# Transposes issued one by one between the weight products, and the weight split one half load further ahead

## The chip, the cores and the metric

The kernel runs on one core of a Trainium2 chip. The metric is the device time of one execution in microseconds (us). TensorE (PE in the profile) multiplies and transposes into the accumulation banks; VectorE (DVE) and ScalarE (ACT) work on rows and banks; GpSimd (POOL) makes masks and scales a few tiles; SyncE (SP) issues the weight transfers. Each engine runs its own list of instructions in order, and they meet at semaphores.

## The reference

256 tokens of width 2048 pass through four layers in float32. The first block is a mixer and a feed-forward; the second is a gated delta net and a band attention:

```python
h = rms_norm(x, g);  proj = h @ w_in                      # 2048 x 9216
merged = g_a * (gmlp(uv) @ w_branch[:1024]) + g_b * (attn(q, k, v) @ w_branch[1024:])
x = x + merged @ w_out
up = conv3(rms_norm(x, g) @ w_up)                         # 2048 x 11008
x = rms_norm(x + (silu(gate) * val) @ w_down)
h = x + gated_deltanet(rms_norm(x)) @ w_out_a             # w_in 2048 x 8224, 16 heads of 128
h = h + chunk_band_attention(rms_norm(h)) @ w_out_b       # w_in 2048 x 8192
```

Nearly all arithmetic is in the products with the weights; attention, the delta rule, the convolutions and the norms are small beside them.

## The kernel before

**The stream of weights.** All weights are cut into tiles of 512 output columns, and each tile into half loads of up to two blocks of 128 rows (`stream_plan`). SyncE brings each half load into one of 4 `raw` slots. ACT rounds it to `w_hi` (line 416), DVE forms the rest `w_lo` (line 426), and TensorE makes three products for each block and each of two token halves: `x_hi*w_lo`, `x_hi*w_hi`, `x_lo*w_hi` (lines 447 to 449), so 12 products of 512 columns in a half load of two blocks. There are 4 slots of `w_hi` and `w_lo` (`SPLIT`): ACT may split half load m only when TensorE is done with m-4. TensorE accumulates tile t in one pair of `gemm` banks while ACT and DVE read the other.

**Side work.** Between half loads each engine does the rest of the kernel. It is written as generators ("sides") that stop at `yield`; one stretch up to a `yield` is called a stage here. `run(half, 8, side)` does a half load and then one stage of each side, eight times. On TensorE a stage is typically eight transposes of 128x128 (`turn_rows`, lines 1638 to 1645; `up_side`, `attend`, `conv_side`, `band` have their own loops), one semaphore increment behind the last of them, and a wait in front. They write the four `aux` banks; ACT and DVE copy these out in the stages after.

**How far apart the engines are.** ACT and DVE do `LOOK` = 2 half loads before their first stage. So their stage s stands behind half load s+2 of the same run of the loop, while TensorE's stage s stands behind its half load s. ACT's split of half load s+2 in turn needs TensorE to be done with s-2.

**The places that the prediction names.** `up_side` (lines 1798 to 1808): eight transposes of `up_rows` in the first stage of a tile. `delta` (lines 1871 to 1881): four stages in a row with eight transposes each, of `tmp`, `q_rows`, `k_rows`, `tmp`; each waits for the copies of the last one (DVE line 1378, ACT line 836) and for the scaled rows that DVE makes right behind its copy (line 1315). Still `delta`: the rows `o_rows` (DVE line 1450) are turned at line 1976 at the end of a group. There are four groups of heads, three of them in a loop. At the start, `hT_lo` (DVE line 1062) of each quarter of the input has to be there before the half loads that read it (lines 1676 to 1682). `load_bias` (line 613) lets ACT issue eight transfers at one place early on. `attend` and `band` turn the attention weights.

Of the kernel before, what the change touches and what calls it, by code (L numbers as in the profile page):

```python
# [24 lines left out]
TB = T // P  # L25
# [23 lines left out]
LOOK = 2  # L49
# [73 lines left out]
def program(nc, ins, out, parts=4):  # L123
    last_tile = {1: T_UP1, 2: T_A, 3: T_B, 4: N_TILES}[parts]
    last_half = TILE_END[last_tile - 1]
    with ExitStack() as ctx:
# [1505 lines left out]
        def _(pe):  # L1632
            pl = Place()
            half = lambda: pe_half(pe, pl)
# [12 lines left out]
            def x_turned(j, s, i):  # L1647

                b = 2 * s + i
                if b >= 4 or j:  # L1650
                    pe.wait_ge(S("hT_lo_done"), 8 * j + b - 3 if b >= 4 else 8 * j)
                turn_rows(x, (b % 4,), "hT_turned", 2 * b)

            def turn_x(j, s, t):

                yield
                pe.wait_ge(S("read_out0"), t + 1)
                pe.wait_ge(S("read_out1"), t + 1)
                x_turned(j, s, 0)
                x_turned(j, s, 1)  # L1660
                yield
                yield
                yield
# [8 lines left out]
            for s in range(2):  # L1672
                pe.wait_ge(S(f"x_landed{s}"), 16)
                for i in range(2):
                    x_turned(0, s, i)
            for load in range(4):
                if load < 2:
                    pe.wait_ge(S(f"x_landed{load + 2}"), 16)
                    for i in range(2):
                        x_turned(0, load + 2, i)  # L1680
                pe.wait_ge(S("hT_lo_done"), 2 * load + 2)
                run(half, 2)

            def mixing():
# [15 lines left out]
                for b in range(4):  # L1700
                    if b >= 2:
                        pe.wait_ge(S("ya_lo"), b - 1)
                    turn_rows(ug, (2 + b % 2,), "ya_turned", 2 * b)
                    yield

            def attend(g):
                for pr in range(4):
# [19 lines left out]
                    for a in range(2):  # L1727
# [5 lines left out]
                        m.then_inc(S("na_p_turned"), 1)  # L1733
# [3 lines left out]
                    for a in range(2):  # L1737
                        h = 2 * pr + a
                        for tb in range(TB):
                            for kb in range(TB):  # L1740
                                m = MM(AX[2 + a][:, tb * NAD:(tb + 1) * NAD], pT[:, a, kb, tb * P:(tb + 1) * P],  # L1741
                                       va[:, kb, h * NAD:(h + 1) * NAD], start=kb == 0, stop=kb == TB - 1)
                    m.then_inc(S("na_pv"), 1)
                    yield
                pe.wait_ge(S("na_out"), 4 * g + 4)
                turn_rows(yb, (2, 3), "yb_turned")
# [4 lines left out]
            def qkv_side(g, part):  # L1751
# [8 lines left out]
                turn_rows(qkv_tok, (0, 1), "qk_turned")  # L1760
# [21 lines left out]
            def turn_merged(n):  # L1782
                yield
                pe.wait_ge(S("merged"), n + 1)
                for b in (2 * n, 2 * n + 1):
                    if b >= 4:
                        pe.wait_ge(S("merged_lo"), b - 3)
                    turn_rows(ga, (b % 4,), "merged_turned", 2 * b)
# [9 lines left out]
            def up_side(t, n, width=2):  # L1798
# [3 lines left out]
                for b in range(2):  # L1802
# [4 lines left out]
                    m.then_inc(S("up_turned"), 1)  # L1807
# [34 lines left out]
            def conv_side(gi, part):  # L1842
# [8 lines left out]
                for i in range(2):  # L1851
                    turn_rows(tok, (i,), "c_turned", 2 * i)
# [5 lines left out]
                for tb in range(TB):  # L1858
                    for h in range(HG):
                        m = turn(AX[tb][:, h * P:(h + 1) * P], xc[:, h, tb * P:(tb + 1) * P], ident[:, :])  # L1860
                m.then_inc(S("c_back"), 1)
# [9 lines left out]
            def delta(gi):  # L1871
# [3 lines left out]
                for j, src in enumerate((tmp, qs, ks, tmp)):  # L1875
# [4 lines left out]
                    turn_rows(src, (2, 3), "d_turned")  # L1880
# [95 lines left out]
                turn_rows(o_rows, (2, 3), "d_y_turned")  # L1976
# [68 lines left out]
            def rows_side(gi, part):  # L2045
# [10 lines left out]
                turn_rows(tok, (0, 1), "b_turned")  # L2056
# [3 lines left out]
            def band(gi):  # L2060
                for _ in range(8):
                    yield
                for pr in range(2):
# [18 lines left out]
                    for a in range(2):  # L2082
# [4 lines left out]
                        m.then_inc(S("b_p_turned"), 1)  # L2087
# [13 lines left out]
                turn_rows(by, (2, 3), "b_y_turned")  # L2101
# [48 lines left out]
```

## Time and profile before

| | |
|---|---|
| median of 3 executions | 2628.32 us (2624.26 to 2629.22) |
| the profiled execution: first to last instruction (span) | 2623.4 us |
| what lies around the span, to the median | 4.9 us |
| TensorE busy | 2558.3 us, 98% |
| products with weights | 9480 of TensorE's 13782 instructions |
| instructions that multiply with `ident` (transposes) | 958 |
| DVE, ACT busy | 1493.5 us (57%), 1211.2 us (46%) |
| granted TensorE clock, mean | 0.993 |

The profiled execution has no timed value of its own beside its span, so the span is set against the median of the three timed ones. The profile's ends of matmuls are modelled: a product of 512 columns is shown with 0.39 us, though the next starts about 0.23 us after it. What an instruction costs TensorE is therefore read from one start to the next, never from its duration.

### The profile page before, as it was taken

What the parts mean: (1) busy time and instruction counts of PE and PEld (TensorE: products, weight loads), DVE (VectorE), ACT (ScalarE), POOL (GpSimd) and SP (SyncE); (2) the same over time, 40 slices, a digit from 0 to 9 for tenths busy, and PEclk for the clock granted to TensorE, in tenths of its full rate; (3) what the DMA queues carried; (4) which work ended last, traced back from release to release, by engine and by line L of the source; (5) the groups of instructions that cost most, each with busy time, mean ns of one, the idle gap of its engine ahead of it and who ended that gap; (6) DMA issues with size and microseconds to landing.
All of it is one profiled execution on the core that took longest, in us unless ns stands there. A gap on an engine that the chain in (4) does not pass through costs nothing.

```text
span 2623.4 us, 38136 instructions
## 1 busy us (share of the span) xinstructions
PE 2558.3 (98%) x13782; PEld 2096.0 (80%) x13782; DVE 1493.5 (57%) x1953; ACT 1211.2 (46%) x1830; POOL 106.2 (4%) x112
## 2 busy tenths in 40 slices
PE   7899999999999999999999999999999999999999
PEld 6688888888888888888887787877877678888887
DVE  5556555555666644666655655556473455555654
ACT  4435444444555533555444635335352335555543
POOL 0101100000200000000000110001101000000000
PEclk9899999999999999999999999999999999999999
DMA  7666555555656565555555433334332366556554
GB/s 243 192 192 161 165 180 186 181 191 192 215 177 188 178 198 194 180 182 181 180 188 161 145 98 113 108 101 123 104 114 73 96 190 189 156 177 190 158 179 161
DMA packets 286901, 431.40 MB, mean 164 GB/s; under 512 B 32560, under 2 KB 126000, under 8 KB 286640
## 3 DMA queue, kind: packets, MB, share of 16 engines
q1 hardware_dynamic: 264064, 414.25, 51.2%
q10 hardware_dynamic: 22704, 15.28, 2.2%
q8 instruction: 95, 1.56, 0.2%
q14 instruction: 38, 0.31, 0.0%
HBM read 427.37 MB, written 7.08 MB: 166 GB/s over the span
## 4 chain that ended last, share of the span: by engine, by line
PE 92%; DVE 3%; ACTq 1%; issue 1%; ACT 1%; DMA 1%; DVEq 0%; SPq 0%
PE gemm L447 27%; PE gemm L448 26%; PE gemm L449 26%; PE aux L1644 2%; PE aux L1924 1%; PE aux L1914 1%; PE aux L1923 1%; DVE w_lo L426 1%; PE aux L1967 1%; PE aux L1970 1%; PE aux L1806 1%; PE aux L1966 1%; DMA bbias<-band_bias_copies 1%; PE aux L1741 1%; ACTq L620 1%
## 5 line engine op out<-in xcount | busy, mean ns | idle before, releaser
L426 DVE TENSOR_TENSOR w_lo<-raw,w_hi 128x1024 fp32r<-128x1024 f32 (+1 forms) x800 | 967.4, 1221 | 607.4 <-ACT w_hi L416 597.9
L416 ACT ACTIVATE w_hi<-raw 128x1024 fp32r<-128x1024 f32 (+1 forms) x800 | 820.7, 1041 | 579.7 <-PE gemm L449 500.2
L447 PE MATMUL gemm<-w_lo,hT_hi 128*128 128x512 f32 (+1 forms) x2304 | 916.8, 398 | 19.3 <-DVE w_lo L426 18.6
L448 PE MATMUL gemm<-w_hi,hT_hi 128*128 128x512 f32 (+1 forms) x2304 | 897.3, 389 | 0.0
L449 PE MATMUL gemm<-w_hi,hT_lo 128*128 128x512 f32 (+1 forms) x2304 | 896.9, 389 | 0.0
L447 PEld LDWEIGHTS gemm<-w_lo,hT_hi 128*128 128x128 f32 x2304 | 434.2, 188 | 118.2 <-DVE w_lo L426 16.1
L449 PEld LDWEIGHTS gemm<-w_hi,hT_lo 128*128 128x128 f32 x2304 | 434.0, 188 | 91.7
L448 PEld LDWEIGHTS gemm<-w_hi,hT_hi 128*128 128x128 f32 x2304 | 434.7, 189 | 83.7
L447 PE MATMUL gemm<-w_lo,yT_hi 128*128 128x512 f32 x472 | 187.0, 396 | 0.8 <-DVE w_lo L426 0.8
L449 PE MATMUL gemm<-w_hi,yT_lo 128*128 128x512 f32 x472 | 186.4, 395 | 0.0
L448 PE MATMUL gemm<-w_hi,yT_hi 128*128 128x512 f32 x472 | 186.4, 395 | 0.0
L447 PE MATMUL gemm<-w_lo,zT_hi 128*128 128x512 f32 x256 | 105.1, 411 | 2.8 <-DVE zT_lo L1458 2.8
L447 PEld LDWEIGHTS gemm<-w_lo,yT_hi 128*128 128x128 f32 x472 | 88.6, 188 | 22.7 <-DVE w_lo L426 1.2
L449 PEld LDWEIGHTS gemm<-w_hi,yT_lo 128*128 128x128 f32 x472 | 88.6, 188 | 21.5
L448 PEld LDWEIGHTS gemm<-w_hi,yT_hi 128*128 128x128 f32 x472 | 88.6, 188 | 21.1
L448 PE MATMUL gemm<-w_hi,zT_hi 128*128 128x512 f32 x256 | 102.5, 400 | 0.0
L449 PE MATMUL gemm<-w_hi,zT_lo 128*128 128x512 f32 x256 | 102.3, 399 | 0.0
L1250 DVE TENSOR_TENSOR x_rows<-x_rows,gemm 128x512 f32<-128x512 f32 x40 | 25.7, 684 | 75.2 <-PE gemm L449 75.2
L1345 DVE SCALAR_TENSOR_TENSOR conv<-aux,conv_taps,conv 128x253 f32<-128x253 f32 (+1 forms) x144 | 62.5, 476 | 8.1 <-issue 6.1
L849 ACT ACTIVATE inverse<-aux 128x512 f32<-128x512 f32 x16 | 9.6, 599 | 117.7 <-PE aux L1924 117.7
L447 PEld LDWEIGHTS gemm<-w_lo,zT_hi 128*128 128x128 f32 x256 | 49.0, 191 | 15.2 <-DVE zT_lo L1458 3.0
L757 ACT ACTIVATE up_rows<-gemm,rstd 128x512 f32<-128x512 f32 (+1 forms) x22 | 15.0, 681 | 94.3 <-PE gemm L449 94.3
(298 smaller groups left out, 2187.1 us busy)
## 6 DMA issues: line engine op xcount, KB each, us to landing
raw<-in_w_up SPq DMA_DIRECT2D x336, 256.0 KB, 3.3
raw<-in_w_in SPq DMA_DIRECT2D x144, 512.0 KB, 4.3
raw<-in_a_w_in SPq DMA_DIRECT2D x128, 512.0 KB, 3.7
raw<-in_b_w_in SPq DMA_DIRECT2D x128, 512.0 KB, 4.1
raw<-in_w_down SPq DMA_DIRECT2D x76, 512.0 KB, 4.5
raw<-in_w_branch SPq DMA_DIRECT2D x32, 512.0 KB, 4.4
raw<-in_w_out SPq DMA_DIRECT2D x32, 512.0 KB, 4.3
raw<-in_a_w_out SPq DMA_DIRECT2D x32, 512.0 KB, 3.7
```

What stands on the lines that cost most here:

```text
L416: nc.scalar.activation(hi, src, ACT.Copy).then_inc(S("hi_done"), 1)
L426: nc.vector.tensor_tensor(lo, src, hi.bitcast(F32), ALU.subtract).then_inc(S("lo_done"), 1)
L447: nc.tensor.matmul(dst, xh, wl[:, k, :], start=h["start"] and k == 0, stop=False)
L448: nc.tensor.matmul(dst, xh, wh[:, k, :], start=False, stop=False)
L449: mm = nc.tensor.matmul(dst, xl, wh[:, k, :], start=False, stop=h["stop"] and k == h["n"] - 1)
L620: act.dma_start(bias[a * GRID:(a + 1) * GRID, u % BR, h, :, :], src).then_inc(S(f"bias_landed{u % BR}"), 16)
L1345: i = V.scalar_tensor_tensor(out=xc[:, 2 * b + e, back:], in0=src[:, 0:T - back], scalar=ctap[:, tap, bass.ds(gi * HG + (part * H + 2 * b ...
L1644: m = turn(AX[b][:, e * T + tb * P:e * T + (tb + 1) * P], src[:, tb, c:c + P], ident[:, :])
L1741: m = MM(AX[2 + a][:, tb * NAD:(tb + 1) * NAD], pT[:, a, kb, tb * P:(tb + 1) * P], va[:, kb, h * NAD:(h + 1) * NAD], start=kb == 0, stop=k ...
L1806: m = turn(AX[b][:, e * T + tb * P:e * T + (tb + 1) * P], ut[:, tb, c:c + P], ident[:, :])
L1914: m = MM(AX[2][rows_, c * C:(c + 1) * C], ATl[rows_, c, :], Tm[rows_, c, :], start=True, stop=True)
L1923: MM(AX[2][rows_, c * C:(c + 1) * C], Um[rows_, c, :], W1[rows_, c, :], start=True, stop=True)
```

## The change

Three things are changed.

`pe_half` takes the sides with it. After every single product it takes one step of each side (`slip`); what is left after the last product of the half load is done behind it. The generators now yield `True` after each transposition (and after each product of `attend`'s second part) and a bare `yield` still ends a stage. So a transposition stands behind the first product, the next behind the second, and so on.

`run` gives no side to its first half load, a stage to each following one, and does the last stage behind the last. So stage s is now spread over half load s+1; what is not a transposition (the small products of `delta`, the scores) still stands together, behind the first product of that half load.

`LOOK` is 3: ACT and DVE have half load s+3 behind them when they come to stage s.

```diff
-LOOK = 2
+LOOK = 3
...
-        def pe_half(pe, pl):
+        def pe_half(pe, pl, sides=()):
...
+            between = list(sides)
+
+            def slip():
+
+                between[:] = [s for s in between if next(s, None)]
+
...
                     nc.tensor.matmul(dst, xh, wl[:, k, :], start=h["start"] and k == 0, stop=False)
+                    slip()
                     nc.tensor.matmul(dst, xh, wh[:, k, :], start=False, stop=False)
+                    slip()
                     mm = nc.tensor.matmul(dst, xl, wh[:, k, :], start=False, stop=h["stop"] and k == h["n"] - 1)
-            mm.then_inc(S("half_done"), 1)
+                    if k == h["n"] - 1 and tb == TB - 1:
+                        mm.then_inc(S("half_done"), 1)
+                    slip()
+            while between:
+                slip()
...
+            def run(half, halves, *sides):
+
+                for i in range(halves):
+                    half(sides if i else ())
+                for s in sides:
+                    while next(s, None):
+                        pass
...
             def turn_rows(src, banks, event, at=0):
 
+                left = 4 * len(banks)
                 for i, b in enumerate(banks):
                     for e in range(2):
                         for tb in range(TB):
                             c = (at + 2 * i + e) * P
                             m = turn(AX[b][:, e * T + tb * P:e * T + (tb + 1) * P], src[:, tb, c:c + P], ident[:, :])
+                            left -= 1
+                            if left:
+                                yield True
                 m.then_inc(S(event), 1)
```

The callers of `turn_rows` become `yield from turn_rows(...)`, and the loops with transposes of their own get a `yield True` behind each.

The first place is TensorE in the loop over the tiles of `w_up`, around the first stage of a tile. Before:

```order
L449 MATMUL gemm<-w_hi,hT_lo 128x512
L1799 REGISTER_ALU
L1806 MATMUL aux<-ident,up_rows 128x128 [waits read_out1,read_out0]
L1806 MATMUL aux<-ident,up_rows 128x128 x7
L439 REGISTER_ALU
L447 MATMUL gemm<-w_lo,hT_hi 128x512 [waits lo_done]
L448 MATMUL gemm<-w_hi,hT_hi 128x512
```

And now, where the waits of the side stand behind the first product of the half load:

```order
L439 REGISTER_ALU
L453 MATMUL gemm<-w_lo,hT_hi 128x512 [waits lo_done]
L1829 REGISTER_ALU
L1836 MATMUL aux<-ident,up_rows 128x128 [waits read_out1,read_out0]
L455 MATMUL gemm<-w_hi,hT_hi 128x512
L1836 MATMUL aux<-ident,up_rows 128x128
L457 MATMUL gemm<-w_hi,hT_lo 128x512
L1836 MATMUL aux<-ident,up_rows 128x128
L453 MATMUL gemm<-w_lo,hT_hi 128x512
L1836 MATMUL aux<-ident,up_rows 128x128
```

The eight transposes stood together between two half loads; now each has a product on either side, and the eighth stands behind the eighth of twelve products.

The second place is TensorE in `delta`, where the transposes of `q_rows` follow those of `tmp`. Before, twelve products stood between the last of `tmp` and the first of `q_rows`, of which the last three are shown:

```order
L447 MATMUL gemm<-w_lo,hT_hi 128x512
L448 MATMUL gemm<-w_hi,hT_hi 128x512
L449 MATMUL gemm<-w_hi,hT_lo 128x512
L1876 REGISTER_ALU
L1644 MATMUL aux<-ident,q_rows 128x128 [waits d_out1,d_out0,d_rows]
L1644 MATMUL aux<-ident,q_rows 128x128 x7
```

Now these stand between them:

```order
L1665 MATMUL aux<-ident,tmp 128x128
L457 MATMUL gemm<-w_hi,hT_lo 128x512
L453 MATMUL gemm<-w_lo,hT_hi 128x512
L455 MATMUL gemm<-w_hi,hT_hi 128x512
L457 MATMUL gemm<-w_hi,hT_lo 128x512
L439 REGISTER_ALU
L453 MATMUL gemm<-w_lo,hT_hi 128x512 [waits lo_done]
L1911 REGISTER_ALU
L1665 MATMUL aux<-ident,q_rows 128x128 [waits d_out1,d_out0,d_rows]
```

Five products are left between the last transposition of one stage and the first of the next.

The third place is DVE at the start, where the splits of the first half loads and the quarters of `hT_lo` take turns. Before:

```order
L426 TENSOR_TENSOR w_lo<-raw,w_hi 128x1024 [waits hi_done] x2
L1050 BN_STATS x_stats<-x_rows 128x6 [waits x_landed0]
L1050 BN_STATS x_stats<-x_rows 128x6
L426 TENSOR_TENSOR w_lo<-raw,w_hi 128x1024 [waits hi_done] x2
L1062 SCALAR_TENSOR_TENSOR hT_lo<-aux,gains,hT_hi 128x256 [waits hT_hi_done]
```

Now:

```order
L426 TENSOR_TENSOR w_lo<-raw,w_hi 128x1024 [waits hi_done] x3
L1062 BN_STATS x_stats<-x_rows 128x6 [waits x_landed0]
L1062 BN_STATS x_stats<-x_rows 128x6
L426 TENSOR_TENSOR w_lo<-raw,w_hi 128x1024 [waits hi_done] x2
L1074 SCALAR_TENSOR_TENSOR hT_lo<-aux,gains,hT_hi 128x256 [waits hT_hi_done]
```

Five splits stand ahead of the second quarter of `hT_lo` instead of four, seven instead of six ahead of the third, nine instead of eight ahead of the fourth. The fifth is the first whose slot TensorE has to free.

## Rows read from the trace of the kernel before

**Rows 1.** The page: busy time, share of the span and instructions
```profile
PE 2558.3 (98%) x13782; PEld 2096.0 (80%) x13782; DVE 1493.5 (57%) x1953; ACT 1211.2 (46%) x1830; POOL 106.2 (4%) x112
```
**Rows 2.** The page: the chain that ended last, by engine
```profile
PE 92%; DVE 3%; ACTq 1%; issue 1%; ACT 1%; DMA 1%; DVEq 0%; SPq 0%
```
**Rows 3.** Waits of PE: who waited for whom, us in total, times, longest
```profile
PE gemm L447 <- DVE w_lo L426: 19.4, 5, 11.9
...
PE aux L1644 <- DVE q_rows L1315: 7.1, 4, 2.2
...
PE aux L1644 <- DVE o_rows L1450: 3.6, 4, 1.4
```
**Rows 4.** Timeline, 681.5 to 685.1 us: start, duration, engine (PEld: weight load), what
```profile
681.63 0.39 PE L447 MATMUL gemm<-w_lo,hT_hi 128*128 128x512 f32 x1
681.63 0.19 PEld L448 LDWEIGHTS gemm<-w_hi,hT_hi 128*128 128x128 f32 x1
...
682.31 1.03 PE L1806 MATMUL aux<-ident,up_rows 128*128 128x128 f32 x8
683.10 0.48 PE L447 MATMUL gemm<-w_lo,hT_hi 128*128 128x512 f32 x1
683.41 0.39 PE L448 MATMUL gemm<-w_hi,hT_hi 128*128 128x512 f32 x1
...
685.03 0.39 PE L449 MATMUL gemm<-w_hi,hT_lo 128*128 128x512 f32 x1
```
**Rows 5.** Instructions of PE that read ident, whole span: busy us (count), clock, DMA
```profile
0.00:2623.40 2623.40, 128.69 (x958) 0.99 0.54 164
```
**Rows 6.** Timeline of PE, 208.6 to 210.6 us: products of 64 moving columns
```profile
209.34 1.45 PE L1741 MATMUL aux<-v_rows,pT 128*128 128x64 f32 x12
```
**Rows 7.** Timeline of PE, 2235 to 2237 us: four of 128 and four of 256 columns
```profile
2235.25 1.47 PE L2077 MATMUL aux<-bkT,bqT 128*128 128x128 f32 x8
...
2236.79 0.39 PE L448 MATMUL gemm<-w_hi,hT_hi 128*128 128x512 f32 x1
```
**Rows 8.** Timeline of DVE in delta, 1487 to 1491.1 us, with idle time before
```profile
1487.44 0.69 DVE L1378 COPY qnT<-aux 128x512 f32<-128x512 f32 x1
1488.05 1.22 DVE L1315 TENSOR_TENSOR k_rows<-k_rows,row_squares 128x1024 f32<-128x1024 f32 x1
```
**Rows 9.** Timeline of PE at the same place
```profile
1486.31 1.09 PE L1644 MATMUL aux<-ident,q_rows 128*128 128x128 f32 x8 [1.87 <-DVE q_rows L1315]
...
1490.01 1.03 PE L1644 MATMUL aux<-ident,k_rows 128*128 128x128 f32 x8
```
**Rows 10.** Timeline of ACT ahead of the transposes of o_rows
```profile
1620.65 1.04 ACT L416 ACTIVATE w_hi<-raw 128x1024 fp32r<-128x1024 f32 x1
```
**Rows 11.** Timeline of DVE at the same place
```profile
1621.73 1.23 DVE L426 TENSOR_TENSOR w_lo<-raw,w_hi 128x1024 fp32r<-128x1024 f32 x1 [2.30 <-ACT w_hi L416]
...
1623.95 2.19 DVE L1450 SCALAR_TENSOR_TENSOR o_rows<-o_rows,o_squares,silu_z 128x128 f32<-128x128 f32 x8 [0.16 <-issue]
```
**Rows 12.** Timeline of PE at the same place
```profile
1625.06 0.39 PE L449 MATMUL gemm<-w_hi,hT_lo 128*128 128x512 f32 x1
1626.19 0.87 PE L1644 MATMUL aux<-ident,o_rows 128*128 128x128 f32 x6 [0.75 <-DVE o_rows L1450]
```
**Rows 13.** Timeline of ACT at the start
```profile
30.07 1.06 ACT L416 ACTIVATE w_hi<-raw 128x1024 fp32r<-128x1024 f32 x1 [1.09 <-PE gemm L449]
```
**Rows 14.** Timeline of DVE at the start
```profile
33.88 1.23 DVE L426 TENSOR_TENSOR w_lo<-raw,w_hi 128x1024 fp32r<-128x1024 f32 x1 [0.70 <-ACT w_hi L416]
35.02 1.66 DVE L1062 SCALAR_TENSOR_TENSOR hT_lo<-aux,gains,hT_hi 128x256 fp32r<-128x256 f32 x4
```
**Rows 15.** Timeline of ACT around load_bias, 86 to 103 us (ACTq: its issues)
```profile
87.81 14.13 ACTq L620 DMA_DIRECT2D bias<-na_bias_copies  x8
102.04 1.06 ACT L416 ACTIVATE w_hi<-raw 128x1024 fp32r<-128x1024 f32 x1 [13.63 <-issue]
```
**Rows 16.** Timeline of PE behind it
```profile
104.42 0.79 PE L447 MATMUL gemm<-w_lo,hT_hi 128*128 128x512 f32 x1 [11.87 <-DVE w_lo L426]
```

More of the change, by code:

```diff
@@ L1633, in _ @@
             pl = Place()
-            half = lambda: pe_half(pe, pl)
+            half = lambda sides=(): pe_half(pe, pl, sides)
             none = iter(())
+            def run(half, halves, *sides):
[4 more added lines that the diff above has]
+                        pass
             MM, turn = nc.tensor.matmul, nc.tensor.transpose
             def turn_rows(src, banks, event, at=0):
+                left = 4 * len(banks)
                 for i, b in enumerate(banks):
@@ L1651, in x_turned @@
                     pe.wait_ge(S("hT_lo_done"), 8 * j + b - 3 if b >= 4 else 8 * j)
-                turn_rows(x, (b % 4,), "hT_turned", 2 * b)
+                yield from turn_rows(x, (b % 4,), "hT_turned", 2 * b)
             def turn_x(j, s, t):
@@ L1658, in turn_x @@
                 pe.wait_ge(S("read_out1"), t + 1)
-                x_turned(j, s, 0)
-                x_turned(j, s, 1)
+                yield from x_turned(j, s, 0)
+                yield True
+                yield from x_turned(j, s, 1)
                 yield
@@ L1674, in _ @@
                 for i in range(2):
-                    x_turned(0, s, i)
+                    finish(x_turned(0, s, i))
             for load in range(4):
@@ L1679, in _ @@
                     for i in range(2):
-                        x_turned(0, load + 2, i)
+                        finish(x_turned(0, load + 2, i))
                 pe.wait_ge(S("hT_lo_done"), 2 * load + 2)
@@ L1702, in mixing @@
                         pe.wait_ge(S("ya_lo"), b - 1)
-                    turn_rows(ug, (2 + b % 2,), "ya_turned", 2 * b)
+                    yield from turn_rows(ug, (2 + b % 2,), "ya_turned", 2 * b)
                     yield
@@ L1732, in attend @@
                                          sc[:, a, tb, kb * P:(kb + 1) * P], ident[:, :])
-                        m.then_inc(S("na_p_turned"), 1)
+                                if kb == TB - 1 and tb == TB - 1:
+                                    m.then_inc(S("na_p_turned"), 1)
+                                yield True
                     yield
@@ L1745, in attend @@
                 pe.wait_ge(S("na_out"), 4 * g + 4)
-                turn_rows(yb, (2, 3), "yb_turned")
+                yield from turn_rows(yb, (2, 3), "yb_turned")
                 yield
@@ L1759, in qkv_side @@
                     pe.wait_ge(S("qk_out1"), 2 * g + part)
-                turn_rows(qkv_tok, (0, 1), "qk_turned")
+                yield from turn_rows(qkv_tok, (0, 1), "qk_turned")
                 yield
@@ L1787, in turn_merged @@
                         pe.wait_ge(S("merged_lo"), b - 3)
-                    turn_rows(ga, (b % 4,), "merged_turned", 2 * b)
+                    yield from turn_rows(ga, (b % 4,), "merged_turned", 2 * b)
+                    if b == 2 * n:
+                        yield True
                 yield
@@ L1806, in up_side @@
                             m = turn(AX[b][:, e * T + tb * P:e * T + (tb + 1) * P], ut[:, tb, c:c + P], ident[:, :])
-                    m.then_inc(S("up_turned"), 1)
+                            if e == width - 1 and tb == TB - 1:
+                                m.then_inc(S("up_turned"), 1)
+                            yield True
                 yield
@@ L1851, in conv_side @@
                 for i in range(2):
-                    turn_rows(tok, (i,), "c_turned", 2 * i)
+                    yield from turn_rows(tok, (i,), "c_turned", 2 * i)
+                    yield True
                 yield
@@ L1879, in delta @@
                         pe.wait_ge(S("d_out1"), gi * 4 + j)
-                    turn_rows(src, (2, 3), "d_turned")
+                    yield from turn_rows(src, (2, 3), "d_turned")
                     yield
@@ L1975, in delta @@
                 pe.wait_ge(S("d_y"), gi + 1)
-                turn_rows(o_rows, (2, 3), "d_y_turned")
+                yield from turn_rows(o_rows, (2, 3), "d_y_turned")
                 yield
@@ L2055, in rows_side @@
                     pe.wait_ge(S("b_out1"), n)
-                turn_rows(tok, (0, 1), "b_turned")
+                yield from turn_rows(tok, (0, 1), "b_turned")
                 yield
@@ L2086, in band @@
                                 m = turn(AX[2 + a][:, (kb + tb) * P:(kb + tb + 1) * P], bsc[:, a, tb, kb * P:(kb + 1) * P], ident[:, :])
-                        m.then_inc(S("b_p_turned"), 1)
+                                if kb == tb == TB - 1:
+                                    m.then_inc(S("b_p_turned"), 1)
+                                yield True
                     yield
@@ L2100, in band @@
                 pe.wait_ge(S("b_y"), gi * 2 + 2)
-                turn_rows(by, (2, 3), "b_y_turned")
+                yield from turn_rows(by, (2, 3), "b_y_turned")
                 yield
```

3 lines of the change are left out of this document (added).

## The prediction

> **What bounds the kernel.** I read the page's busy times first: TensorE is busy 2558.3 of 2623.4 us, DVE 57%, ACT 46% [rows 1]. The chain of what ended last says the same from the other side: 92% of it is TensorE [rows 2]. So only two things can change the time: what TensorE's own instructions cost it, from one start to the next, and the places where it stands still. The waits of TensorE, third, name the places: 19.4 us for splits of weights, 11.9 of them at one place, 7.1 us for `q_rows` in four waits, 3.6 us for `o_rows` in four [rows 3]. The rest is many small ones. A change that puts transposes elsewhere must therefore make a transposition cheaper, or remove waits, and must not make new ones.
>
> **What a transposition costs now.** In the timeline of TensorE the products with the weights follow each other by 0.227 us (three from 681.63 to 682.31). Eight transposes start at 682.31, one product follows, and the next product starts at 683.41: 1.10 us, less one product 0.873 us, so 109 ns each [rows 4]. Not all is paid there: up to the product at 685.03 eight products have started since 682.31 and 2.72 us have passed, so the burst has cost 2.72 - 8 x 0.227 = 0.904 us, 113 ns for each transposition. The extra 31 ns is spread over the products behind the burst.
>
> What sets the 109 ns? Either the load of the next 128 columns of stationary data or the stream of moving data. Both have a row. Products with only 64 moving columns, in a row: 12 in 1.45 us, and less the 0.27 us by which one outlasts its start (1.03 - 7 x 0.109 in rows 4) that is 1.18 us for eleven steps, 107 ns each, so half the moving columns save nothing: the load sets it [rows 6]. And four products of 128 and four of 256 columns take 1.54 us up to the second product behind them, less 0.227 us: 1.31 us for twelve times 128 columns, 109 ns each, so 128 float32 columns stream for about as long as a load takes [rows 7]. Finally the load for a product starts when the product ahead of it starts, 681.63 and 681.63 in the trace, not earlier [rows 4].
>
> **Part A, one by one.** Between two products, the load for the transposition hides behind the first product. But then the load for the second product can start only when the transposition starts, and it takes the same 107 to 109 ns. I see no way for a transposition to cost less than in the burst: what is exposed is only another load. On top comes what the burst paid once. The first product behind it starts the next 6 to 9 ns late, and up to 31 ns are lost until the rhythm is back; now a change between the two kinds comes sixteen times where it came twice. Of 958 transposes [rows 5] I count in the new order 92 that still stand in bursts (start, first tiles, the end of a run), so 866 are moved. Bounds: if no load were exposed and the moving columns ran at the products' rate, 128/512 of 0.227 us = 57 ns, 56 ns less than now, -48 us. If each paid the whole 31 ns by itself, +27 ns on seven of eight, +23 us. I take +6 ns, the nearest row being the product behind a burst: +5.2 us.
>
> The Trainium skill ("TensorE: Matmul & The Clock Gate", section "Step-by-step: what each phase is for") says that TensorE pulls weight loads ahead of running matmuls within a window of 64 instructions when they go to the background weight buffer. Taken freely, with more than one load ahead, that would hide the load behind the neighbouring product, and it is the first rival's mechanism. The same page, section "LDWEIGHTS (loading the stationary operand)", prices a load at the number of columns / 1.2, 107 ns for 128; by that alone each transposition costs at least 107 ns wherever it stands, as in my sum, and the trace's 107 to 109 ns agree.
>
> **Part B, later events in `delta`.** A burst sent its semaphore 0.9 us behind the half load. Now the eighth transposition starts behind eight products and seven transposes, 8 x 0.227 + 7 x 0.109 = 2.58 us, and the wait of the next stage stands behind 13 products and 8 transposes, 3.82 us. Between them are 1.24 us. What has to happen there is in the trace: the last of a burst starts at 1486.31 + 1.09 - 0.27 = 1487.13, DVE copies at 1487.44 and has scaled the next rows at 1488.05 + 1.22 = 1489.27, 2.14 us later [rows 8, 9]. The products covered that (the next transposes start at 1490.01 with no idle time before them). Now 0.9 us are late. This holds for the `k_rows` and the second `tmp` stage, and about half of it for the stage behind them, which needs the copy and a shorter operation. The wait for `q_rows` stays as it is, 1.87 us, since there DVE is late by its own work. 2.3 us in a group, four groups: +9.4 us. Bounds: 0, if DVE gets ahead elsewhere, and +13 if the fourth stage pays in full and `q_rows` is later too.
>
> In `attend` the same calculation passes: only a copy of about 0.7 us stands between the transposes and the next stage. I put it at 0, with up to +4 us if DVE is held up by a split there.
>
> **Part C, LOOK in chains that a split holds.** DVE's stage s now stands behind the split of half load s+3, and ACT may make that one only when TensorE is done with s-1 instead of s-2. Where DVE or ACT waits for a transposition of the stage anyway this costs nothing. Where a chain is tight it does: ahead of the transposes of `o_rows` ACT rounds weights at 1620.65 [rows 10], DVE follows at 1621.73 and makes `o_rows` from 1623.95 to 1626.14 [rows 11], and TensorE waits from 1625.29 to 1626.19 [rows 12]. The half load then running began 12 x 0.227 = 2.72 us before 1625.29, at 1622.57, and with the new order the rounding may not start before that: 1.9 us later. The wait itself moves by one product, 0.23 us. +1.6 us in each group of the loop, taken as +4.5 us for three. Bounds 0 and +6.5 (all four).
>
> At the start it is the same. A quarter of `hT_lo` now follows the split of a half load whose slot comes free one half load later. From the end of that half load: rounding 1.06 us [rows 13], rest 1.23, `hT_lo` 1.66 [rows 14], together 3.95 us against the 2.72 us in which TensorE does its next one. +1.2 us for the third and the fourth quarter, +1.0 us for the second: +3.4 us, bounds 0 and 4.
>
> **Part D, what LOOK gives.** ACT issues eight transfers for 14.13 us and rounds nothing [rows 15]; TensorE uses up what is split and stands for 11.87 us [rows 16]. One more half load is split by then: -2.7 us, bounds 0 and that. The other four waits for splits are 7.5 us together [rows 3]; most end a chain that the lead doesn't shorten, so I take -1 us (0 to -5). SyncE's queue is hardly touched: a `raw` slot comes free by the same split as before.
>
> **Sum.** 5.2 + 9.4 + 4.5 + 3.4 - 2.7 - 1 = +18.8 us on a span of 2623.4 us. The median lies 4.9 us above the span and I keep that distance: 2647 us, 0.7% slower. About 0.2%, 5.3 us, is what a measurement of this kernel can tell from no change.
>
> **Rivals.** (1) The loads hide. TensorE loads ahead across a short matmul, a transposition between two products costs 57 ns, and the gain decides from the point where more than 19 us of the 48 come true. With parts B to D unchanged: 2647 - 5 - 48 = 2594 us, faster. For it: in the trace a load is never exposed beside a product of 512 columns. Against it: the start of the load together with the product before it, and 109 ns for twelve streams of 128 columns [rows 4, 7]. 10%.
> (2) It evens out. DVE and ACT, idle near half the time, absorb the later events, transposes cost 113 ns as before, and only part D and half of the start remain: 2618 to 2633 us, at 2628. For it: they have idle time; against it: the sums of B and C are over by 0.9 and 1.6 us, not by a hair. 22%, of that 6 faster, 14 without a change, 2 slower.
> (3) The alternation never lets TensorE find its rhythm: the +23 us of part A. 2665 us, with B and C at their ends 2671. 12%.
> My forecast, 2636 to 2660, has 56%.
>
> The range is 2616 to 2672: down to the whole of part D with nothing lost, up to rival 3 with its ends; the first rival is left out. The likeliest case's own range is 2634 to 2664. Faster by over 0.2%: 10 + 6 = 16%; within: 14%; slower: 56 + 12 + 2 = 70%.
>
> **What would show it.** In the new profile, in the tiles of `w_up`, twelve products and eight transposes from one half load to the next: 3.60 to 3.66 us is right, 3.2 us is rival 1, over 3.8 us rival 3. In the waits of TensorE: new ones for `k_rows` and `tmp` of near 1 us each in `delta`, `o_rows` from 3.6 to about 8 us, the long wait for a split 9.2 us instead of 11.9, and waits of about 1 us for `hT_lo` in the first 45 us. If the starts of product and transposition stand 57 ns apart beyond a product's own 0.227 us, the argument on loads is wrong and the sum with it. The granted clock should stay at 0.99.

## The result, and the profile after

| | before | after |
|---|---|---|
| median | 2626.29 us (2623.6 to 2629.22, 4 runs) | 2657.35 us (2655.71 to 2658.72, 4 runs) |
| ratio | | 1.0117, 95% interval 1.0103 to 1.0131 |
| span of the profiled execution | 2623.4 us | 2657.0 us |
| granted clock, mean | 0.993 | 0.990 |

The changed kernel is 31 us slower. The page of the profile after, its busy times and its chain, which answer to [rows 1, 2]:

```profile
PE 2574.4 (97%) x13782; PEld 2081.7 (78%) x13782; DVE 1504.2 (57%) x1953; ACT 1235.2 (46%) x1830; POOL 104.2 (4%) x112
...
PE 92%; DVE 3%; ACT 2%; ACTq 1%; issue 1%; DMA 1%; DVEq 0%; SPq 0%
```

The instructions are the same in number and TensorE still bounds the kernel, so the 33.6 us between the spans are TensorE's own again: dearer starts, or places where it stands. Its waits (who waited for whom, us in total, times, longest), which answer to [rows 3]:

```profile
PE gemm L453 <- DVE w_lo L426: 15.3, 3, 10.1
PE aux L1665 <- DVE q_rows L1327: 8.9, 4, 2.9
...
PE aux L1665 <- DVE tok L1478: 5.5, 1, 5.5
PE aux L1665 <- DVE tmp L1327: 5.2, 5, 2.4
PE aux L1665 <- DVE o_rows L1462: 3.6, 4, 1.6
...
PE aux L1836 <- DVE up_rows L1298: 2.7, 1, 2.7
PE gemm L453 <- DVE hT_lo L1074: 2.6, 2, 1.3
...
PE aux L1665 <- DVE k_rows L1327: 2.3, 3, 0.8
PE gemm L453 <- DVE zT_lo L1633: 1.6, 1, 1.6
```

Splits fell from 19.4 to 15.3 us. `q_rows` rose from 7.1, `tok` from 3.0 and `tmp` of the scaling from one wait of 1.4 us to five, and `k_rows`, `up_rows`, `zT_lo` of line 1633 and `hT_lo` in front of a product are new. `o_rows` did not move.

To see where the time goes, the start of the same weight product is compared in both traces. What that lag grows by in each stretch (times of the kernel before), worked out from the starts of the product at either end of it:

| stretch, us before | what is there | lag grows by |
|---|---|---|
| 0 to 72 | start, `hT_lo` | +4.3 |
| 72 to 114 | ACT's bias transfers | -2.7 |
| 114 to 385 | mixer and `attend` | +2.0 |
| 385 to 1270 | `w_out`, tiles of `w_up` | +0.7 |
| 1270 to 1417 | last, narrow tile of `w_up`, `w_down` | +1.2 |
| 1417 to 1471 | last norm, start of the delta net's stack | +8.9 |
| 1471 to 1606 | first group of `delta` | +6.1 |
| 1606 to 1916 | the same stretch of two further groups | +3.1 each |
| 1916 to 2084 | last group and end of the delta net | +3.7 |
| 2084 to the end | band attention | +3.2 |

**The starts.** TensorE in the half load with the transposes of `up_rows`; the place answers to [rows 4]. Columns: start, duration, engine, what.

```profile
708.95 0.39 PE L453 MATMUL gemm<-w_lo,hT_hi 128*128 128x512 f32 x1
...
709.21 0.48 PE L455 MATMUL gemm<-w_hi,hT_hi 128*128 128x512 f32 x1
...
709.55 0.48 PE L457 MATMUL gemm<-w_hi,hT_lo 128*128 128x512 f32 x1
...
712.63 0.40 PE L453 MATMUL gemm<-w_lo,hT_hi 128*128 128x512 f32 x1
```

From 709.21 to 709.55 is one product and one transposition, 0.34 us where a product alone takes 0.227. The half load takes 712.63 - 708.95 = 3.68 us. With the burst it was 12 x 0.227 + 0.904 = 3.63. From one tile to the next the lag of the two traces grows by 0.065 us, 8 ns for each of eight transposes.

**In `delta`.** TensorE in the second group, the first transposition of `k_rows`, the last of these, and the first of `tmp` (in brackets: idle time before, and who ended it):

```profile
1667.18 0.33 PE L1665 MATMUL aux<-ident,k_rows 128*128 128x128 f32 x1 [0.75 <-DVE k_rows L1327]
...
1669.64 0.27 PE L1665 MATMUL aux<-ident,k_rows 128*128 128x128 f32 x1
...
1671.83 0.33 PE L1665 MATMUL aux<-ident,tmp 128*128 128x128 f32 x1 [0.75 <-DVE tmp L1327]
```

And DVE there:

```profile
1669.95 0.69 DVE L1390 COPY knT<-aux 128x512 f32<-128x512 f32 x1 [1.41 <-PE aux L1665]
1670.56 1.22 DVE L1327 TENSOR_TENSOR tmp<-q_rows,exp_gc 128x1024 f32<-128x1024 f32 x1
```

One turn of this ring is 4.65 us: 2.46 from the first to the last transposition of `k_rows`, 2.19 for copy, scaling and the way back. Before, one stage took 1490.01 - 1486.31 = 3.70 us [rows 9], set by twelve products and a burst, because the burst's seven steps of 0.109 and the same 2.2 us made only 3.0. So a stage that needed 0.76 us from first to last transposition now needs 2.46, and here it stands in a ring. The table of waits has `k_rows` three times for four groups: in the last group the transposes of `q_rows` end a run of the loop and still stand together, and that wait is absent.

**Where a term was missed.** ACT, and DVE below it, ahead of the narrow last tile of `w_up`:

```profile
1275.28 1.06 ACT L416 ACTIVATE w_hi<-raw 128x1024 fp32r<-128x1024 f32 x1 [2.39 <-DMA raw<-in_w_down]
...
1277.51 0.48 DVE L1298 TENSOR_SCALAR up_rows<-gemm,rstd 128x256 f32<-128x256 f32 x1
```

With `LOOK` 3 the reading of the tile stands behind the split of one more half load, the first of that size of `w_down`, and its transfer has not landed (in brackets, the 2.39 us that ACT waited for it). TensorE waits 2.67 us for `up_rows`, and behind the wait, from 1278.13 on, it runs slowly:

```profile
1278.81 0.41 PE L1836 MATMUL aux<-ident,up_rows 128*128 128x128 f32 x1
1279.45 0.41 PE L1836 MATMUL aux<-ident,up_rows 128*128 128x128 f32 x1
```

A product and a transposition take 0.64 us here, not 0.34. The window there (stretch: length, PE busy, count, granted clock, DMA share, GB/s) gives the reason:

```profile
1278.10:1281.30 3.20, 3.17 (x10) 0.53 0.72 205
```

The clock is at the lower of its two levels, 1.2 instead of 2.4 GHz, for about 3 us behind that stand. Over the whole span the mean of 0.990 instead of 0.993 means 2 x (0.010 x 2657 - 0.007 x 2623) = some 16 us more at the lower level. A stretch at half the clock costs at most half its length, so by this estimate the clock is at most 8 of the 33.6 us.

### The profile page after: what moved, and what is told of

Same layout as the page of the kernel before. It is cut to its first block, busy times and chain, and to the rows that moved or that the text cites. A ratio compares the mean times of both kernels' runs of the same rounds, so it can differ in the third digit from the quotient of the medians.

```text
span 2657.0 us, 38136 instructions
## 1 busy us (share of the span) xinstructions
PE 2574.4 (97%) x13782; PEld 2081.7 (78%) x13782; DVE 1504.2 (57%) x1953; ACT 1235.2 (46%) x1830; POOL 104.2 (4%) x112
## 4 chain that ended last, share of the span: by engine, by line
PE 92%; DVE 3%; ACT 2%; ACTq 1%; issue 1%; DMA 1%; DVEq 0%; SPq 0%
PE gemm L455 26%; PE gemm L453 26%; PE gemm L457 26%; PE aux L1665 2%; PE aux L1959 1%; PE aux L1949 1%; PE aux L1958 1%; DVE w_lo L426 1%; PE aux L2002 1%; PE aux L1836 1%; PE aux L2005 1%; ACT w_hi L416 1%; PE aux L2001 1%; ACTq L632 1%; DMA bbias<-band_bias_copies 1%
## 5 line engine op out<-in xcount | busy, mean ns | idle before, releaser
L416 ACT ACTIVATE w_hi<-raw 128x1024 fp32r<-128x1024 f32 (+1 forms) x800 | 832.3, 1043 | 830.3 <-PE gemm L457 790.0
L453 PE MATMUL gemm<-w_lo,hT_hi 128*128 128x512 f32 (+1 forms) x2304 | 918.5, 399 | 19.0 <-DVE w_lo L426 15.3
L455 PE MATMUL gemm<-w_hi,hT_hi 128*128 128x512 f32 (+1 forms) x2304 | 933.9, 405 | 0.0
L457 PE MATMUL gemm<-w_hi,hT_lo 128*128 128x512 f32 (+1 forms) x2304 | 924.7, 401 | 0.0
L455 PEld LDWEIGHTS gemm<-w_hi,zT_hi 128*128 128x128 f32 x256 | 49.3, 192 | 12.8 <-issue 0.4
L457 PEld LDWEIGHTS gemm<-w_hi,zT_lo 128*128 128x128 f32 x256 | 49.1, 192 | 11.9
```

Of the source, the lines that this page charges most:

```text
L416: nc.scalar.activation(hi, src, ACT.Copy).then_inc(S("hi_done"), 1)
```

## The experiments

The runs share two groups of measurements of the kernel before, and one of its own for the last: 2625.26 us for the first four, 2624.11 for the next four, 2623.55 for the ninth. The lags are from one profiled execution of each kernel, and the lower clock falls elsewhere in each; one such stretch moves a lag by up to 3 us (experiment 9 has an example).

### 1. One by one, without the longer lead

```diff
-LOOK = 3
+LOOK = 2
```

> The changed kernel with LOOK back at 2, so the order one by one alone. Theory (the later events in delta and the alternation are paid by the order itself, LOOK adds the waits at the start and in chains that a split holds): + 7 us for 866 transposes at 8 ns, + 11 us for the waits in delta, the first wait for a split back at its full length, so about 2645 us, 18 us over before and 12 us under the changed kernel. Rival 1 (LOOK = 3 makes nearly all of the loss): within 5 us of before, 2626 to 2631. Rival 2 (the order needs the lead, without it ACT and DVE come late with the splits): slower than the changed kernel, over 2660.

2650.67 us, 1.0098 (1.0082 to 1.0113). The waits:

```profile
PE gemm L453 <- DVE w_lo L426: 22.3, 6, 11.6
...
PE aux L1665 <- DVE q_rows L1327: 8.8, 4, 2.9
...
PE aux L1665 <- DVE k_rows L1327: 2.3, 3, 0.8
```

Everything in `delta` is as in the changed kernel, +3.1 us of lag for each further group, so that belongs to the order. The new waits for `hT_lo` and `up_rows` are gone, and the long wait for a split is back at 11.6, so those belong to `LOOK`. The loss without the lead was larger than I had put it, by 6 us. Part of it is at the start of the delta net: between 1417 and 1471 us the lag grows by 5.2 us here too, though the wait for `tok` is down to 0.2 us; TensorE waits for splits (1.7 and 2.2 us) and for `w_ab_lo` (1.3 us) instead.

### 2. The longer lead, with bursts

The kernel before with `LOOK` = 3.

> The kernel before with LOOK = 3 and the transposes in bursts as they were. Theory: + 4.4 us in the first 48 us, - 2.6 us at the transfers of the bias, and 2 to 8 us of waits where a chain of ACT and DVE stands behind a split (start of the delta net, last narrow tile): 2630 to 2637. Rival 1 (LOOK makes nearly all of the loss): 2650 or more. Rival (LOOK pays for itself in bursts): 2626 or less.

2638.89 us, 1.0058 (1.0045 to 1.0072), just above what I expected. The waits:

```profile
PE gemm L447 <- DVE w_lo L426: 12.9, 2, 8.9
PE aux L1644 <- DVE q_rows L1315: 9.1, 4, 2.7
...
PE aux L1644 <- DVE tok L1466: 6.7, 1, 6.7
...
PE gemm L447 <- DVE hT_lo L1062: 2.6, 2, 1.3
PE aux L1806 <- DVE up_rows L1286: 2.5, 1, 2.5
```

The waits for splits are 6.5 us shorter, and the kernel still loses 13 us, so 19.5 are lost in all: 2.6 for `hT_lo`, 2.5 for `up_rows`, 3.7 more for `tok`, 2.0 more for `q_rows`, 2.5 more for `tmp`. These sum to 13.3; some 6 us are in none of them. So the lead does harm where ACT and DVE make something that TensorE needs soon and now have one more split in front of it. The two halves of the change are 25 and 13 us by themselves and 31 together. They overlap in `delta`: `q_rows` is 9 us in all three, and from 1471 to 1916 us the lag grows by 5.9 us with the lead alone and by 12.2 both with the order alone and with the whole change.

### 3. `delta`'s four stages in bursts

```diff
-                    yield from turn_rows(src, (2, 3), "d_turned")
+                    finish(turn_rows(src, (2, 3), "d_turned"))
```

> The changed kernel, but the four stages of eight transposes in a row of delta stand in one piece behind the first product of their half load; all other transposes stay one by one. Theory: the waits for k_rows, the second tmp and the stage behind them go (2.75 us in each of four groups), and 128 transposes less pay 8 ns: 2657 - 11 - 1 = 2645. Rival (the waits come from LOOK, since DVE's scaling stands behind one more split): they stay at 1 us each, 2655 to 2658.

2652.56 us, 1.0109 (1.0094 to 1.0125). The wait for `k_rows` is gone, yet the median is only 5 us below the changed kernel's and not 12, and the intervals of the two ratios overlap, so even the 5 are not sure. `q_rows` stays at 8.9 us, `tmp` is still 4.4, and one wait is new:

```profile
PE gemm L453 <- ACT tok L898: 1.7, 1, 1.7
```

The ring in the middle of a group is cut: the lag grows by 1.1 and 1.8 us in the two further groups instead of 3.1. What is left is as much as those two groups lose in experiment 2, so the ring by itself costs 2.0 and 1.2 us in them, and the rest of what these groups lose stays without it. Whether that is the lead's is not settled by this run (experiment 9 has nearly the same without it).

### 4. Two by two

`slip` still runs after every product, but the generators stop only after every second transposition.

> The changed kernel, with two transposes between products instead of one, in all stages of eight but those of band's attention weights. Theory (what alternation costs is paid at each change between the two kinds, and the delta waits depend on how many products stand ahead of the last transposition): a stage of eight costs 0.03 us less of changes, - 3.5 us, and the last transposition starts four products earlier, which removes nearly all of the 11 us in delta: about 2644. Rival (each transposition between products costs its 8 ns, however they are grouped): the tile of w_up keeps 12 products and 8 transposes at 3.66 us, and 2647 or more.

2642.86 us, 1.0071 (1.0058 to 1.0085): 12 us (by the ratios) to 15 us (by the medians) faster than one by one, with the same lead. In `w_up`:

```profile
707.92 0.48 PE L455 MATMUL gemm<-w_hi,hT_hi 128*128 128x512 f32 x1
708.23 0.38 PE L1837 MATMUL aux<-ident,up_rows 128*128 128x128 f32 x2
...
709.28 0.47 PE L455 MATMUL gemm<-w_hi,hT_hi 128*128 128x512 f32 x1
```

From 707.92 to 709.28 are three products and six transposes: 1.36 - 0.68 = 0.68 us, 113 ns each, the price in the burst. The last of eight now stands behind four products, the wait for `k_rows` is gone, and a further group costs 1.5 us. Two terms of the sum come to as much, 866 x 8 ns = 6.9 us of part A and 4 x (3.1 - 1.5) = 6.4 us of part B, but the traces do not put all of it there. Their spans differ by 18.1 us: 3.2 in the two further groups, 4.5 in the first, 3.8 between 1417 and 1471 us, the other 6.6 spread over the rest. Of the 18 us that remain against the kernel before, the lead's are 13 if it costs beside pairs what it costs beside bursts (experiment 2).

### 5. What stands between two products

The kernel before; in two half loads of each looped tile of `w_up` there are eight useless products, each behind one product with a weight: 64, 128 or 256 moving columns with 128 stationary ones, or 128 moving and 32 stationary. They are in the number format of the weights and not float32.

> The kernel before, with eight additional products of no use in each of two half loads of every looped tile of w_up, each behind one product with a weight: stationary columns x moving columns 128x64 and 128x256 in the one tile, 128x128 and 32x128 in the other, all in the weights' number format. Read from start to start. Theory (the load for the product behind is exposed, and only one load is ever ahead): 128x64 and 128x128 cost the same, 107 to 118 ns, since the product behind loads 128 columns whatever the short one does; 32x128 costs the same too; 128x256 costs 113 to 120 ns, its own stream. Rival (loads hide across a short product): 27 ns for 64 moving columns, 53 ns for 128, 107 ns for 256. Both say nothing on the whole time but that it is 25 us or so longer than before.

TensorE with 64 columns, and with 256:

```profile
690.60 0.48 PE L458 MATMUL gemm<-w_hi,hT_hi 128*128 128x512 f32 x1
690.91 0.19 PE L449 MATMUL aux<-hT_lo,hT_hi 128*128 128x64 f32 x1
690.91 0.19 PEld L460 LDWEIGHTS gemm<-w_hi,hT_lo 128*128 128x128 f32 x1
...
691.97 0.47 PE L460 MATMUL gemm<-w_hi,hT_lo 128*128 128x512 f32 x1
...
697.07 0.40 PE L458 MATMUL gemm<-w_hi,hT_hi 128*128 128x512 f32 x1
...
698.84 0.40 PE L456 MATMUL gemm<-w_lo,hT_hi 128*128 128x512 f32 x1
```

Four pairs in 1.37 us and five in 1.77 us: less the product's 0.227, 115 ns with 64 columns and 127 with 256. Over all half loads of the kind 115, 114 and 126 ns for 64, 128 and 256 columns, and 115 ns with 32 stationary columns; for 256 I had expected 120 at most. So neither the moving columns up to 128 nor the size of its own load matter. What is paid is the load of 128 columns for the product behind it, which starts only when the short one starts (both at 690.91). The first rival, hidden loads, would have shown 27 ns for 64 columns and 53 for 128. A fixed price of any short product, whatever is loaded next, is the other way to read four equal prices. Rows of the changed kernel speak against it, products that load 64 columns and move 32:

```profile
1477.71 0.27 PE L2068 MATMUL aux<-log_decay,m_le 64*64 64x32 f32 x2 [0.85 <-ACT beta L967]
...
1477.94 0.28 PE L2070 MATMUL aux<-log_decay,m_le 64*64 64x32 f32 x2
```

Four of them start in 0.23 us, 57 ns each, half the price with half the columns to load. The one execution of this run took 2654.75 us, 31 longer than before where I had put 25.

The Trainium skill ("TensorE: Matmul & The Clock Gate", section "Step-by-step: what each phase is for") lets weight loads be pulled ahead of running matmuls within a window of 64 instructions. These rows show a lead of one load and no more. The same page's price of a load, columns / 1.2 or 107 ns for 128 (section "LDWEIGHTS (loading the stationary operand)"), agrees with 115 ns less the few ns of a change between kinds.

### 6 and 7. The bias transfers spread, and a later wait

The kernel before, `LOOK` 2, bursts. ACT issues the eight transfers of `load_bias` one in every second half load instead of all at once. In the seventh, DVE's wait for the band's bias is moved besides from the start of the band stack to its first use.

```diff
+                for u in range(BR):
+                    for piece in range(4):
+                        yield
+                        load_bias(u, piece)
+                        yield
...
-                if t == 2:
-                    for u in range(BR):
-                        load_bias(u)
```

> The kernel before, with ACT's first eight transfers of bias issued one in every second half load of the two tiles behind, instead of all eight at one place. Theory (TensorE stands for 11.9 us since ACT rounds nothing while it issues for 14.1 us; spread, 1.8 us of issue fit between two roundings): the wait goes, 2626 - 12 = 2614. Rival (each issue holds ACT up where the lead of two half loads is short, or the bias is then late for the attention): 2620 or more, with new waits for splits up to 180 us.

> As the one before, and DVE waits for the bias of the band attention where it is first used, not at the start of the last part. Theory: the wait of 4.8 us for a split at 2142 us goes too, 2614 - 5 = 2609, and with it a stretch at the lower clock. Rival (DVE's wait only moves to the first scores): 2614.

2610.57 us, 0.9946 (0.9932 to 0.996), and 2607.11 us, 0.9922 (0.9909 to 0.9936); I had expected 2614 and 2609. The two intervals just overlap, so what the seventh wins over the sixth is told by its trace more than by its time. The window of TensorE at the place of [rows 16], in the sixth run:

```profile
86.00:120.00 34.00, 34.00 (x160) 1.00 0.80 254
```

and in the kernel before:

```profile
88.00:122.00 34.00, 22.13 (x86) 0.80 0.62 181
```

The waits for splits in the seventh:

```profile
PE gemm L447 <- DVE w_lo L426: 2.8, 3, 1.7
```

19.4 us of waits for splits are 2.8, and at both places the stretch at the lower clock behind the stand has gone too. Taking these two stalls away at their causes gives 17 us between the medians. The longer lead got 2.7 us out of the first of these places and paid for it in the others. The seventh beats both kernels.

### 8. The wait for `tok` filled

The changed kernel, with twenty useless products of 512 columns ahead of the wait for `tok`, about as long as the wait.

> The changed kernel, with 20 products of 512 columns of no use (4.5 us) ahead of the wait for the first tok rows of the delta net, where TensorE stands for 5.5 us and the clock was granted at half for 10.2 us behind it. Theory (the lower clock follows a long stand of TensorE, and is a part of the loss by itself): the stand shrinks to about 1 us, the half clock behind it goes or shortens, and 2 to 5 us are won: 2653 to 2655. Rival (the clock falls there for another reason, or the products only move the chain): 2657 or more, with 10 us of half clock still there.

2654.83 us, 1.0113 (1.0098 to 1.0129), which can't be told from the changed kernel's 1.0117. In its trace the useless products fill 1426.64 to 1431.36 us; here are the first and the last transposition of `tok`, and the window around them:

```profile
1432.33 0.30 PE L1665 MATMUL aux<-ident,tok 128*128 128x128 f32 x1 [0.97 <-DVE tok L1478]
...
1437.68 0.27 PE L1665 MATMUL aux<-ident,tok 128*128 128x128 f32 x1
...
1426.00:1440.00 14.00, 11.38 (x62) 1.00 0.49 150
```

In the changed kernel:

```profile
1430.87 0.45 PE L1665 MATMUL aux<-ident,tok 128*128 128x128 f32 x1 [5.51 <-DVE tok L1478]
...
1438.78 0.27 PE L1665 MATMUL aux<-ident,tok 128*128 128x128 f32 x1
...
1426.00:1440.00 14.00, 7.94 (x32) 0.63 0.49 148
```

From the first to the last transposition 5.35 us instead of 7.91, with nearly the same waits between them. The lower clock costs 2.6 us at this place; that much is shown by the trace. From 1417 to 1471 us the lag grows by 4.9 us instead of 8.9, but the two spans differ by 1.4 us only, since other stretches of the two executions differ as well. It is too little for the clock to be the cause of the loss.

### 9. One by one everywhere but in `delta`'s four stages, `LOOK` 2

> LOOK is 2 as in the kernel before, and the transposes stand one by one between the products everywhere but in delta's four stages, where they stand in a burst. If the parts add up, what is left is the price of the alternation outside delta (some 780 transposes at 8 ns, 6 us, seen in the w_up tiles as 0.065 us in a half load with eight) and the stages that moved behind a half load (q_rows, end of the band stack, about 3 us): 2633 to 2640 us, with no wait for k_rows and the waits for splits of weights not shorter than before. Rival: the loss of the one-by-one order with LOOK 2 (24 us) is made elsewhere than in delta; then it stays near 2648 us. Third: without delta's part the alternation costs nothing, within 3 us of the kernel before.

2644.48 us, 1.0076 (1.0063 to 1.009). This is between my first and second figure and fits neither. The ring is gone from `delta` (no wait for `k_rows`), but the group still loses 1.5 and 1.8 us; in this trace TensorE waits elsewhere:

```profile
PE gemm L453 <- ACT tok L898: 1.8, 1, 1.8
```

With experiment 1 it says that 6 us of the order's loss (give or take 5, by the two intervals) hang on `delta`'s four stages, and some 20 on all the rest: the starts (738 transposes at 8 ns, 6 us), and later events in front of `q_rows`, at the start of the delta net (3.0 us of lag between 1417 and 1471 us) and at the end of the band stack, where TensorE waits 1.6 us for `zT_lo`. I had looked for later events in one place only. What share each of these has is not separated by a run. Another 3 us of lag near the end of the delta net are only in the profiled execution: TensorE has a granted clock of 0.74 there from 2066 to 2079 us, where experiment 1 has 1.00 with the same waits.

## Why the prediction was right, and where its steps were not

The time, 2657 us, is inside the range and inside the forecast's 2636 to 2660, 10 us above the value. The sum said +18.8 on the span, measured were +33.6. That the time still fell inside 2660 is luck in part. I added 4.9 us from span to median; every timed execution lies 1.7 to 1.8 us above its own span, and the other 3.2 came from a profiled execution that was faster than the median. After the change the profiled execution is the slowest of four, 2657.0 against a median of 2657.35, and with the measured span the same addition would have given 2662. Step by step:

- **Part A, one by one: right, a little small.** 8 ns for each moved transposition instead of 6, so 6.9 us for 866, not 5.2. The price within a half load, 3.68 us, is 0.02 above the interval I named, in which I had not added my own 6 ns with the right weight (3.63 + 8 x 0.006 is 3.68). The +23 us of rival 3 are 27 ns on all 866; on seven of eight, as I wrote, they are 20. The argument on loads holds: experiment 5 shows the exposed load directly, and two by two brings back the burst's price. Rival 1 falls with it, and rival 3's 31 ns on each too.
- **Part B, later events in `delta`: right in mechanism, and the size open between half and the whole.** The waits for `k_rows` and the second `tmp` are there, 0.75 us of standing and 1.02 us longer from start to start. A further group costs 3.1 us, of which some 0.4 belong to part A; 2.7 in place of 2.3, and 10.7 in place of 9.4 if the fourth group, which has no wait for `k_rows`, loses as much (4 x 2.3 is 9.2, a slip of mine). But not all of that is the ring's: without it a further group gets back 2.0 and 1.2 us beside the lead (experiment 3), 1.6 and 1.3 without the lead (experiments 1 and 9). Four times that is 5 to 8 us. That `q_rows` "stays as it is, 1.87 us" was wrong: 2.9 us in the first group, 8.9 in all instead of 7.1, and a stretch at the lower clock behind it. Experiments 1 and 2 show that either half of the change does that.
- **`attend` at 0: inside its bound.** The lag grows by 2.0 us from 114 to 385 us, mixer and attention, starts included; experiment 2 has 0.0 there.
- **Part C, `o_rows`: wrong.** I wrote "with the new order the rounding may not start before that: 1.9 us later". It measured 0: 3.6 us in four waits as before. The rounding at 1620.65 [rows 10] belongs to one half load less far ahead than I took it for, since DVE makes `o_rows` a stage before TensorE turns them. What holds that chain is ACT's own work. In the changed kernel:

```profile
1640.08 1.28 ACT L880 ACT_TABLE_LOAD   x1
...
1641.49 1.04 ACT L416 ACTIVATE w_hi<-raw 128x1024 fp32r<-128x1024 f32 x1
...
1643.42 1.06 ACT L416 ACTIVATE w_hi<-raw 128x1024 fp32r<-128x1024 f32 x1 [0.27 <-PE gemm L457]
```

The rounding at 1641.49 starts when the table load and the root are done, with a free slot. The one that must wait for TensorE is the next, and DVE makes `o_rows` before it comes to that. The row of before had no releaser in brackets behind the rounding, which was the sign that no slot was waited for.

- **Part C, the start: right, a little small.** +3.4 predicted, +4.3 measured, with two new waits for `hT_lo` in front of products, 1.32 us each, of which this is the first:

```profile
35.15 0.50 PE L453 MATMUL gemm<-w_lo,hT_hi 128*128 128x512 f32 x1 [1.32 <-DVE hT_lo L1074]
```

- **Part D: right in sign and mechanism, and closer in number than it deserves.** -2.7 predicted, -2.65 in the lag. The stand itself went from 11.87 to 10.12 us, 1.75 less and not 2.7; the rest came behind it, and no run separates how. Experiments 2 and 3, with the same lead, have stands of 8.9 and 9.0 us and -4.4 and -4.3 in this stretch, and experiment 1, without it, has -1.4. The other waits for splits, for which I took -1 us, went from 7.5 to 5.2, and longer waits for `tok` and `up_rows` took their place; I don't count this term below.

```profile
109.73 0.80 PE L453 MATMUL gemm<-w_lo,hT_hi 128*128 128x512 f32 x1 [10.12 <-DVE w_lo L426]
```

- **Not in the sum at all: some 15 us.** +8.9 between 1417 and 1471 us (the wait for `tok`, 5.5 instead of 3.0 us, waits of 1.2 us for `w_ab_lo` and 0.8 for `beta`, and the lower clock behind them), +1.2 around the narrow tile, some 3 in the first group beyond a later group's, +2.1 at the end. The longer lead moves `tok` (experiments 1 and 2), but it is not alone there: the order without it loses 5.2 us in this stretch and the lead without the order 4.6. Which instruction of the last norm hands the delay on was not tried. I had followed the change through the loops and not through the places between them, where one phase hands over to the next. That the clock "should stay at 0.99" held in two digits and was still an oversight. The low end of my range, 2616, does not follow from part D either: with both of its terms at their ends it is 2620.6.

Together: 6.9 + 10.7 + 4.3 - 2.7 = 19.2 us from terms that the prediction had, for which it gave 15.3, and 15 us from places that it did not look at; that is 34 for 33.6 measured. The sum closes because each stretch is read from the lag and sorted by place; it does not show that the cause named for each place is the whole of it. The direction was well founded, and the 4.5 us for `o_rows` that did not come hid part of what was missing.

## What to carry to other kernels

Spreading small instructions between large ones pays only where the large one hides something of the small one; read first what sets the small one's price, here the load for its neighbour, which cost 113 ns in a burst and no less between products. Then ask for each spread stage how long it now takes from its first to its last instruction, and whether a ring (result, copy, scaling, next stage) is longer than the work that covers it. A longer lead for one stream is a delay for everything else in the same instruction list: look at the places where a phase starts or ends, and remove a stall at its cause before buying cover for it.

## What the hardware showed that I had not expected

- A short product between two of 512 columns costs 114 to 115 ns whether it moves 64 or 128 columns and loads 32 or 128, and only 12 ns more with 256.
- Behind the stand of 2.67 us the window of 3.2 us has a granted clock of 0.53, and the window of 14 us around the stand of 5.51 us has 0.63. Filling the second stand with useless products kept the window at 1.00. The seventh experiment shows it the other way round: the window from 2140 to 2160 us has 0.83 in the kernel before, with a wait of 4.5 us in it, and 1.00 without that wait.
